# The last expert's second layer by column halves, the last norm without GpSimd, and 4 MB weight transfers in six of eight expert groups

## The reference, cut to what matters

```python
def expert_block(args):
    xb, e = args
    hid = xb @ lp["moe_w1"][e] + lp["moe_b1"][e]            # 1024 -> 2048
    gate = jnp.minimum(hid[:, :D_FF], SWIGLU_LIMIT)
    lin = jnp.clip(hid[:, D_FF:], -SWIGLU_LIMIT, SWIGLU_LIMIT)
    act = gate * jax.nn.sigmoid(SWIGLU_ALPHA * gate) * (lin + 1.0)
    return act @ lp["moe_w2"][e] + lp["moe_b2"][e]          # 1024 -> 1024
...
h = layer_norm(DEEPNORM_ALPHA * x + y_mix, lp["ln1_g"], lp["ln1_b"])
out = layer_norm(DEEPNORM_ALPHA * h + moe(h, lp), lp["ln2_g"], lp["ln2_b"])
```

## Time and profile before

| | |
|---|---|
| median of 3 runs | 1108.36 us (1108.23 to 1110.98) |
| profiled execution, its time | 1107.56 us |
| profiled execution, its span from first to last instruction | 1105.8 us |
| TensorE busy | 1068.5 us (97%) |
| VectorE / ScalarE / GpSimd busy | 374.0 / 163.6 / 44.3 us |
| DMA, mean over the span | 385 GB/s, 425.77 MB |
| chain of waits by engine | PE 76%, DMA 21%, DVE 2% |

### The profile page before, as it was taken

One profiled execution on the slowest core, in us unless ns is written; L12 is line 12 of the kernel. 1 busy time (PEld: TensorE's weight loads), 2 busy tenths in 40 slices (PEclk: granted clock), 3 DMA queues, 4 the chain that ended last, 5 costly groups with the idle time before them and its releaser, 6 DMA issues.

```text
span 1105.8 us, 13963 instructions
## 1 busy us (share of the span) xinstructions
PE 1068.5 (97%) x5411; PEld 461.6 (42%) x5411; DVE 374.0 (34%) x939; ACT 163.6 (15%) x314; POOL 44.3 (4%) x103
## 2 busy tenths in 40 slices
PE   7999999999999999999999999999999999999896
PEld 4667554434343433334343333333333333434332
DVE  4697665223231313131414141313232323122134
ACT  4164623000100000001000100010101010100002
POOL 8000310000000000000000000000000000000001
PEclk9999999999999999999999999999999999999998
DMA  9534649999999999999999999999999999999993
GB/s 297 196 142 165 250 161 366 403 425 428 430 427 426 427 429 429 430 427 428 429 430 430 427 428 428 429 430 428 428 427 430 429 430 427 427 429 429 428 426 151
DMA packets 41790, 425.77 MB, mean 385 GB/s; under 512 B 6633, under 2 KB 13166, under 8 KB 17177
## 3 DMA queue, kind: packets, MB, share of 16 engines
q1 hardware_dynamic: 39873, 423.62, 91.4%
q0 software_dynamic: 1888, 1.75, 0.6%
HBM read 423.39 MB, written 2.17 MB: 385 GB/s over the span
## 4 chain that ended last, share of the span: by engine, by line
PE 76%; DMA 21%; DVE 2%; issue 0%; ACT 0%; SPq 0%; DVEq 0%
PE bank L1922 34%; DMA ring<-in_moe_w_dram 21%; PE bank L1937 11%; PE bank L1524 7%; PE bank L1883 6%; PE bank L1896 6%; PE bank L1751 3%; PE bank L1781 2%; PE bank L1551 1%; PE bank L1947 1%; PE bank L1529 1%; PE bank L1891 1%; PE bank L1995 0%; PE bank L1773 0%; PE bank L1744 0%
## 5 line engine op out<-in xcount | busy, mean ns | idle before, releaser
L1922 PE MATMUL bank<-ring,hT 128*64 128x512 f32 x2048 | 455.4, 595 | 16.1 <-DMA ring<-in_moe_w_dram 16.1
L1922 PEld LDWEIGHTS bank<-ring,hT 128*64 128x64 f32 x2048 | 141.5, 137 | 301.0 <-issue 267.1
L1937 PE MATMUL bank<-ring 128*64 128x512 f32 x1024 | 227.0, 595 | 0.7 <-DMA ring<-in_moe_w_dram 0.7
L1416 DVE TENSOR_SCALAR ring<-bank 128x512 f32<-128x512 f32 x32 | 22.1, 692 | 312.2 <-PE bank L1922 312.2
L1937 PEld LDWEIGHTS bank<-ring 128*64 128x64 f32 x1024 | 70.6, 137 | 133.8 <-issue 126.6
L1433 DVE COPY ring<-bank 64x512 f32<-64x512 f32 x32 | 22.2, 694 | 219.9 <-PE bank L1937 219.9
L1883 PEld LDWEIGHTS bank<-ring 128*128 128x128 f32 x744 | 85.4, 192 | 25.2 <-issue 25.2
L1883 PE MATMUL bank<-ring 128*128 128x128 f32 x744 | 91.3, 279 | 0.0
L1365 DVE TENSOR_SCALAR hT<-bank,ring 128x128 f32<-128x128 f32 x128 | 43.6, 402 | 130.9 <-PE bank L1883 130.4
L906 ACT ACTIVATE ring<-ring 128x512 f32<-128x512 f32 x32 | 20.1, 630 | 380.8 <-DVE ring L1416 380.8
L1896 PE MATMUL bank<-ring 128*128 128x512 f32 x128 | 63.5, 618 | 0.0
(11 more groups left out here) (327 smaller groups left out, 618.1 us busy)
## 6 DMA issues: line engine op xcount, KB each, us to landing
ring<-in_moe_w_dram SPq DMA_DIRECT2D x192, 2048.0 KB, 29.5
ring<-in_w_in_dram SPq DMA_DIRECT2D x5, 1536.0 KB, 13.5
ring<-in_w_out_dram SPq DMA_DIRECT2D x2, 2048.0 KB, 11.0
ring<-in_w_in_dram SPq DMA_DIRECT2D x1, 2048.0 KB, 13.2
xt<-in_x_prompt_dram SPq DMA_DIRECT2D x2, 512.0 KB, 3.8
lnbc<-in_ln_g_dram SPq DMA_DIRECT2D x2, 512.0 KB, 12.2
lnbc<-in_ln_b_dram SPq DMA_DIRECT2D x2, 512.0 KB, 12.6
out_dram<-xt SPq DMA_DIRECT2D x4, 256.0 KB, 2.1
```

Source lines behind the costliest of these rows:

```text
L1922: ins = pe.matmul(bank[b][64 * h:64 * h + 64, :], xT[:, q, k, j * CAP:(j + 1) * CAP], ring[:, c:c + 512], start=False, stop=k == KT - 1)
L1937: ins = pe.matmul(bank[OUT_BANK[j]][64 * h:64 * h + 64, :], actT[:, j, k % 4, (k // 4) * CAP:(k // 4 + 1) * CAP], ring[:, c:c + 512], star ...
```

## The change

It has three parts.

1. **Transfers.** In groups 1 to 6, a unit of the first layer is loaded by one transfer of 4 MB in place of two of 2 MB. It is issued when both slots are free, and TensorE waits for all of it before it begins the unit. The second layer keeps 2 MB transfers, and so do groups 0 and 7. The last group's second halves have semaphores of their own (`w1_half_last`).
2. **Last expert.** The last expert's second layer does all 8 steps of column half 0, then the first 4 steps of half 1, then the sums that need only half 0 (sample's first half, parts 0 and 2), then the last 4 steps of half 1, and, after half 1 is copied, the remaining sums. `residual(2)` and `residual(3)` move ahead of the transposes of `put`. For every pair, ScalarE now copies both halves of expert 1 and VectorE both halves of expert 0.
3. **Last norm.** The order of the statistics is parts 0, 2, 4, 1, 3, and the factors are computed after all three variances. VectorE does the gain and the offset of both column halves of the first 128 rows; GpSimd keeps only the sample's. The order of ScalarE's work in the norm stays.

```diff
-LAST_ORDER = (4, 0, 1, 2, 3)
+LAST_ORDER = (0, 2, 4, 1, 3)
...
+        def w1_unit(e, s):
+            return moe_w1[0, bass.ds(e, 1), s * 4 * P:(s + 1) * 4 * P, :].rearrange("a (p t) c -> p (a t c)", t=4)
...
+                            if whole:
+                                src = w1_unit(ei, c)
+                                room(k + 1)
+                                sp.dma_start(slots(k % SLOTS, 2), src).then_inc(w_full[k // 2 % 4], 16)
+                                continue
...
-            with sp.Fori(1, NE // GROUP) as g:
-                load_group(GROUP * g, GROUP * g)
+            with sp.Fori(1, NE // GROUP - 1) as g:
+                load_group(GROUP * g, GROUP * g, whole=True)
...
+            load_group(NE - GROUP, GROUP * whole_groups, half=w1_half_last, at=GROUP)
...
-            pool.wait_ge(ld_ln, 96)
-            pool.wait_ge(y_hat, 1)
-            st.then(pool.tensor_tensor(Y[:, 0, 0:512], Y[:, 0, 0:512], ln2[:, 0, 0:512], ALU.mult))
-            st.do(pool.tensor_tensor(Y[:, 0, 0:512], Y[:, 0, 0:512], ln2[:, 1, 0:512], ALU.add), y_done[0])
...
-                        for j in range(2):
-                            act.wait_ge(w_used, PAIR * pi + 2 * W1P + 2 * j + 2)
-                            act.activation(eout[64 * j:64 * j + 64, 0, :], bank[OUT_BANK[j]][0:64, :], ACT.Copy
-                                           ).then_inc(out_ready, 1)
+                        act.wait_ge(out_half, pi + 1)
+                        act.activation(eout[64:128, 0, :], bank[OUT_BANK[1]][0:64, :], ACT.Copy).then_inc(out_ready, 1)
+                        act.wait_ge(w_used, PAIR * pi + PAIR)
+                        act.activation(eout[64:128, 1, :], bank[OUT_BANK[1]][64:128, :], ACT.Copy).then_inc(out_ready, 1)
...
-                        def expert_out(j):
-                            dve.wait_ge(w_used, PAIR * pi + 2 * W1P + 2 * j + 2)
-                            dve.tensor_copy(eout[64 * j:64 * j + 64, 1, :], bank[OUT_BANK[j]][64:128, :]).then_inc(out_ready, 1)
+                        def expert_out():
+                            dve.wait_ge(w_used, PAIR * pi + 2 * W1P + 2)
+                            for h in range(2):
+                                dve.tensor_copy(eout[0:64, h, :], bank[OUT_BANK[0]][64 * h:64 * h + 64, :]).then_inc(out_ready, 1)
...
+            def gained(h):
+
+                w = slice(h * 512, (h + 1) * 512)
+                dve.wait_ge(y_hat, h + 1)
+                st.do(dve.tensor_tensor(Y[:, 0, w], Y[:, 0, w], ln2[:, 0, w], ALU.mult))
+
+            def offset(h):
+
+                w = slice(h * 512, (h + 1) * 512)
+                st.do(dve.tensor_tensor(Y[:, 0, w], Y[:, 0, w], ln2[:, 1, w], ALU.add), y_done[0])
+
+            half_stats(0, 0)
+            half_stats(1, 0)
             dve.wait_ge(last_summed, LAST_ORDER.index(4) + 1)
             st.do(dve.bn_stats(sq6[:, :], bank[LAST_BANK[4]][:, 0:QD]), sample_stats)
-            half_stats(0, 0)
+            half_stats(0, 1)
             dve.wait_ge(sample_moved, 4)
             variance(2, SAMP, s46[0:SAMP, :, :])
-            half_stats(0, 1)
             st.settle()
             variance(0, P, stat[:, 0, :, :])
-            scale_and_shift(2, SAMP, 0)
-            half_stats(1, 0)
-            scale_and_shift(0, P, 1)
             half_stats(1, 1)
             st.settle()
             variance(1, P, stat[:, 1, :, :])
+            scale_and_shift(2, SAMP, 0)
+            scale_and_shift(0, P, 1)
...
-            w1 = slice(512, D)
-            dve.wait_ge(y_hat, 2)
-            st.then(dve.tensor_tensor(Y[:, 0, w1], Y[:, 0, w1], ln2[:, 0, w1], ALU.mult))
-            st.do(dve.tensor_tensor(Y[:, 0, w1], Y[:, 0, w1], ln2[:, 1, w1], ALU.add), y_done[3])
+            gained(0)
+            gained(1)
+            st.settle()
+            offset(0)
+            offset(1)
...
+                def second_step(j, f, k, h):
+
+                    c = f % 4 * 2 * SLOT + k * D + h * 512
+                    return pe.matmul(bank[OUT_BANK[j]][64 * h:64 * h + 64, :],
+                                     actT[:, j, k % 4, (k // 4) * CAP:(k // 4 + 1) * CAP],
+                                     ring[:, c:c + 512], start=k == 0, stop=k == KT - 1)
...
+                def last_half(f, k0, k1):
+
+                    for k in range(k0, k1):
+                        ins = second_step(1, f, k, 1)
+                        if k % 4 == 3:
+                            ins.then_inc(w_used, 1)
+
+                def last_layer():
+
+                    f = (PAIR * q + 2 * W1P + 2) // 2
+                    for k in range(KT):
+                        if k == 0:
+                            pe.wait_ge(w_full[f % 4], 16 * (gi * 3 + f // 4 + 1))
+                        if k == 4:
+                            pe.wait_ge(w_half[f % 4], 16 * (gi + 3))
+                        ins = second_step(1, f, k, 0)
+                    ins.then_inc(out_half, 1)
+                    last_half(f, 0, 4)
+                    pe.wait_ge(out_ready, n_pass * (4 * PAIRS))
+                    add_sample(0, 2)
+                    add_experts(0)
+                    add_experts(2)
+                    last_half(f, 4, KT)
...
                     residual(0)
                     residual(1)
+                    pe.wait_ge(g1_ready, 2 * pi + 2)
+                    residual(2)
+                    pe.wait_ge(l1_ready, 2 * pi + 2)
+                    residual(3)
...
-            pe.wait_ge(g1_ready, n_pass * NE)
-            pe.wait_ge(l1_ready, n_pass * NE)
-            residual(2)
             pe.wait_ge(out_ready, n_pass * (4 * PAIRS) + 1)
-            add_experts(4)
-            add_experts(0)
+            add_sample(2, 4).then_inc(last_summed, 1)
             add_experts(1)
-            add_experts(2)
-            residual(3)
             add_experts(3)
```

More of the change, by code:

```diff
@@ L323, in build_kernel @@
         w_half = [sem(f"w_half{s}") for s in range(SLOTS // 2)]
+        w1_half_last = [sem(f"w1_half_last{s}") for s in range(SLOTS // 2)]
         w_used = sem("w_used")
@@ L365, in build_kernel @@
         rows_normed, sample_normed = sem("rows_normed"), sem("sample_normed")
-        y_done = [sem(f"y_done{n}") for n in range(4)]
+        y_done = [sem(f"y_done{n}") for n in range(3)]
         ld_lnq = sem("ld_lnq")
@@ L486, in _, with load_group @@
             load_first(2)
-            def load_group(e, n, first=0):
+            def load_group(e, n, first=0, whole=False, half=w_half, at=0):
                 def expert(i):
@@ L506, in load_group @@
                             room(k + 1)
-                            sp.dma_start(slots(k % SLOTS + 1, 1), src[1]).then_inc(w_half[k // 2 % 4], 16)
+                            sp.dma_start(slots(k % SLOTS + 1, 1), src[1]).then_inc(half[k // 2 % 4], 16)
                     for j in range(2):
@@ L1393, in _ @@
             st.then(dve.tensor_scalar(npass_f[:, 0:1], npass_f[:, 0:1], 1.0, None, ALU.add))
-            st.then(dve.tensor_scalar(npass_f[:, 1:2], npass_f[:, 0:1], float(NE // GROUP), -1.0, ALU.mult, ALU.add))
+            st.then(dve.tensor_scalar(npass_f[:, 1:2], npass_f[:, 0:1], float(NE // GROUP), -2.0, ALU.mult, ALU.add))
             st.then(dve.tensor_copy(npass[:, :], npass_f[:, 0:2]), routed)
@@ L1904, in residual, with add_sample, add_experts, pair @@
                               start=True, stop=False)
-            def pair(q, gi, pi, first=False, final=False):
+            def add_sample(q0, q1):
+                for q in range(q0, q1):
+                    ins = pe.matmul(bank[LAST_BANK[4]][SAMP * q:SAMP * q + SAMP, 0:QD], putT[:, 2 * P:2 * P + SAMP],
+                                    eout[:, q // 2, (q % 2) * QD:(q % 2 + 1) * QD], start=False, stop=True)
+                return ins
+            def add_experts(c):
+                pe.matmul(bank[LAST_BANK[c]][:, :], putT[:, c // 2 * P:(c // 2 + 1) * P], eout[:, c % 2, :], start=False, stop=True
+                          ).then_inc(last_summed, 1)
+            def pair(q, gi, pi, first=False, final=False, group=""):
                 def first_layer(j, k0, k1):
@@ L1912, in first_layer @@
                             pe.wait_ge(w_full[f % 4], 16 * (gi * 3 + f // 4 + 1))
-                        if k % 4 == 2:
-                            pe.wait_ge(w_half[f % 4], 16 * (gi * 3 + f // 4 + 1))
+                        if k % 4 == 2 and group == "first":
+                            pe.wait_ge(w_half[f % 4], 16 * (f // 4 + 1))
+                        if k % 4 == 2 and group == "last":
+                            pe.wait_ge(w1_half_last[f % 4], 16 * (f // 6 + 1))
                         if j == 0 and k < 4 and first:
@@ L1933, in second_layer @@
                         if k == 4:
-                            pe.wait_ge(w_half[f % 4], 16 * (gi * 3 + f // 4 + 1))
+                            pe.wait_ge(w_half[f % 4], 16 * (f // 4 + 1 if group == "first" else gi + 3))
                         for h in range(2):
[L1936 to L1939, removed]
```

(28 more changed lines are left out.)

19 lines of the change are left out of this document (9 added, 10 removed).

## The result

The changed kernel takes 1113.4 us (median of 6 runs, 1112.0 to 1114.5) against 1108.6 before: 1.0041 times the time, 95% interval 1.0031 to 1.0051. It is slower by 4.8 us; 1114.7 was forecast, 6.3 more than before. The profiled execution, the fastest of the six, took 1111.98 us with a span of 1110.2, against 1107.56 and 1105.8 for the one before. The last 2 MB transfer ahead of the first 4 MB one is issued at 246.0 in both traces, so times of the two can be set side by side.

What follows compares the result with a forecast made beforehand. Transfers set the experts' pace, then the path from the last pair's matmuls to the end; last expert +6.4, norm +2.8, packets -2.9 give 1108.4 + 6.3 = 1114.7 us, likeliest case 1112.5 to 1116.5, with bounds 1111.8 to 1119.5.

Steps and rivals of the forecast that it cites:

- Packets: First-layer transfers: larger packets save a cost per packet, 0.061 us for each of 48 merged pairs, 2.9 us in all.
- a last landing 3 us earlier: Expert weight transfers: the last weights land 3 us earlier; its absence was listed as a sign of being wrong.
- It fits by 0.6 us. Cost nothing.: Shallow queue early on: a 4 MB unit issued at 280.8 must begin at 281.4, so no time is lost.
- The rival of the dry queue: Groups 1 and 2: the shallow queue runs dry once or twice, +3 on the forecast, 1117.7 us; chance 0.07.
- 32 records of one half at 0.43: Last expert's second layer on TensorE: 32 records at 0.43 us each make 13.7, 13.5 after corrections.
- the 0.215 of the rival: Last expert: one half of the array alone runs at 0.215 us a record, giving 1109.6 us; chance 0.08.
- less one overlap at the change of half: Last expert's 32 records: one overlap where the halves change takes 0.4 us off their 13.7.
- The landing no longer binds.: Last expert: step 4 comes 1.7 us later in the new order, so TensorE doesn't wait for the last weights.
- Sums and copy: End of last expert: sums of 2.55 us before the last records and 2.55 after, with a 0.9 wait for ScalarE's copy.
- Residuals moved, no cost: Residuals 2 and 3 before the transposes of `put`: take 1.7 us while TensorE idles 1.60 us, so cost nothing.
- The norm, +2.8: Last norm on VectorE: later statistics and factors, a root wait and more operations, less GpSimd's interference, add 2.8 us.
- The stores behind it stay as they are.: End of the kernel, behind VectorE's last norm: the stores are unchanged, so no time is added or saved there.

Runs made afterwards that it cites:

- e1_transfers: The 4 MB first-layer transfers alone, with last expert and norm as in the kernel before: 1105.99 us, 0.9974 times the kernel before.
- e8_best: e1_transfers with group 1 loaded in halves too and residuals 2 and 3 ahead of the transposes of `put`: 1106.4 us, 0.999 times the kernel before.
- e3_alternate: Changed kernel, but the last expert's column halves alternate step by step and all last sums follow both copies: 1108.35 us, 0.9995 times the kernel before.
- e2_tail: Changed kernel with all transfers of 2 MB, so only the new last expert and norm remain: 1115.12 us, 1.0057 times the kernel before.
- e4_factors: Changed kernel with the two `scale_and_shift` moved ahead of the last statistics: 1111.85 us, 1.0028 times the kernel before.
- e7_blocks_of_4: As e3_alternate, but the last expert's halves take turns every 4 steps (8 records): 1108.93 us, run once.

## Why the prediction was right, and where its numbers were off

The direction was as forecast, and so were the mechanism of part 2, which is the costly one, and of the norm: 4.8 us where 6.3 were predicted, 1113.4 inside the likeliest case's own range of 1112.5 to 1116.5. By its own steps:

- **Packets, -2.9 us forecast.** The mechanism is right and e1_transfers measured -2.7, but that the number fits is luck: two errors cancel. The saving for a merged unit is 0.08 us, not 0.061 (0.31 for a pair, not 0.24), which makes 3.7 for all 48; and about 1.2 us are lost on the way, for which the forecast had nothing. The sign "a last landing 3 us earlier" came out as 2.5.
- **"It fits by 0.6 us. Cost nothing."** This step failed. It allowed 2.3 us from the issue of a unit to its first byte. The first unit and the third are issued when the transfer in front has 2.9 and 3.2 us to go, and both land 13.4 us after their issue, 3.7 more than the 9.7 that 4 MB take; they come 0.8 and 0.5 us late. The rival of the dry queue, with 1 to 3 us, was nearer for this place. But it isn't shown to be the whole: e8_best has no unit behind a shallow queue and loses no less over the run.
- **32 records of one half at 0.43.** No row of the kernel before shows this term: its records of the two column halves alternate, 0.43 us for two, 10.52 for 48, hence the 0.215 of the rival, and 0.43 for one alone was the author's estimate. The changed kernel shows it, with single loads 0.43 us apart from 1078.88 to 1081.88. So it was right in the pace, and e3_alternate gives all of it back: 5.05 us of the medians. The size was off: "less one overlap at the change of half" should have been four records. In the changed kernel the records take (1088.40 - 1079.3) + 3.65 = 12.7 us (they begin 16 records of 0.215 behind 1075.82) instead of 13.5, although a wait of 0.3 for the landing at 1083.05 is in it.
- **"The landing no longer binds."** Half right: the load at 1083.05 was idle for 1.03 us, where 0.29 is usual. The matmul of the load at 1081.88 starts at 1082.31, and the next matmul at 1083.05: 0.74 later and not 0.43, so TensorE waits 0.3 us. e2_tail, where that load was idle for 0.35, bears it out: its 40 records take 12.29 us, not 12.65. The transfers gained 2.5, but TensorE, whose residuals start 3.1 earlier, gained more.
- **Sums and copy.** 2.47 and 2.53 against 2.55 each, and a wait of 0.68 against 0.9. Right. That the array's tiling changes was the author's reason for counting all of the 0.57, and no run shows it; what they show is that the 4 records of half the sample's sums take 1088.95 - 1088.40 = 0.55 us, where all 8 took 0.57. Part 2 as a whole: +5.3 against +6.4, mostly for the four records that ran side by side.
- **Residuals moved, no cost.** Right: `put`'s transposes follow at 1070.64 without a wait.
- **The norm, +2.8.** Right: +2.93. The forecast wait of 1.2 for the root is 1.13. VectorE's first L1485, 1.22 us instead of 0.75, runs beside GpSimd's L667 (0.72 us from 1102.43), which the terms did not hold; the last statistics begin 1098.48 - 1097.73 = 0.75 after the matmul, 0.8 forecast.
- **"The stores behind it stay as they are."** Off by 0.7 us in the change's favour: the span goes on for 2.5 us behind VectorE instead of 3.2. The stores did stay; SyncE's wait at the end of the program fell from 1.0 to 0.2 us, in every kernel with the new norm (e2_tail, e3_alternate and e4_factors too) and in no trace of the old one (before, e1_transfers). Why the new norm shortens it is open.

## What to carry to other kernels

Here matmuls with weight tiles of 128x64 ran two at a time only while the two column halves took turns closely, in blocks of at most 4 records: 48 records in 10.52 and 10.57 us. Before reordering such records for the sake of an earlier copy, count the weight loads: two for each 0.43 us went with 0.215 us for a record, one for each 0.43 us with 0.43. And moving work ahead of a wait won only the wait, here 0.6 us. An order that gives a chain of small operations a new place should be priced on the other engine: four operations of 0.15 us, put behind the last statistics, cost VectorE a wait of 1.1 us for ScalarE. Where transfers set the pace, larger packets gained (0.08 us for each 4 MB), and the same merging without larger packets did not.

## What the runs showed of the hardware

- TensorE does not keep to the program's order between the two column halves. It starts up to 4 records of the other half early: blocks of 4 records run wholly side by side (10.57 us for 48, as with 10.52 when they alternate), blocks of 8 in part (12.40), and halves of 16 records each hardly (the changed kernel: 12.7 us for the 32, where 16 x 0.43 = 6.9 would be side by side). In strict order, by the estimate under e7_blocks_of_4, blocks of 4 would take 3.9 us more than alternating records, and they took 0.05 more. The ends of matmuls are modelled in the profile and say nothing.
- A 4 MB unit of 32 KB packets takes 0.08 us less than two transfers with 16 KB packets, at 431 against 429 GB/s; a merged transfer with the old packets takes as long as two.
- Landings in a full queue are not all even. Before the change, the transfer issued at 959.4 lands 5.85 us after the one in front, where 4.89 is usual; the unit issued at 370.6 in the changed kernel lands 10.15 after, and the first one of e8_best 10.35, where 9.72 is usual. The cause is open, and a single late landing, such as e8_best's first, can't be put down to its place in the order.
- A program's last wait can hide a microsecond: SyncE waits 1.0 us at the end of the kernel before and 0.2 us at the end of the changed one, with all stores landed.
